# Down projection of a one-core decoder layer: the last pair of output tiles in block products too

## The chip, the cores and the metric

The kernel runs on one core of one Trainium2 chip. The metric is the device time of one execution in microseconds (us). Three executions of the kernel before took 895.30, 895.37 and 896.08 us; the median is 895.37 us.

## What is computed

The reference is one layer of a decoder: two token mixers side by side, then a convolutional FFN, for 512 prompt tokens and 8 sample tokens together (520 columns in the kernel). The change lies in the last part:

```python
a, gval = jnp.split(conv, 2, axis=-1)
x = x + (jax.nn.silu(a) * gval) @ w_down      # w_down: 2816 x 1024
...
y_prompt = rmsnorm(xp, g_final)
y_sample = rmsnorm(xs, g_final)
```

Everything is float32. The final RMS norm needs the sum of squares of each token over all 1024 features, so no output can be scaled before the last feature tile is finished.

## The kernel before

Activations lie feature-major: a tile is 128 features by 520 tokens, and the 1024 features make 8 tiles (`KT`). The down projection contracts 2816 hidden features, 22 k tiles (`FT`). Each 128 x 128 weight block is split in a high part (`whi`, written by ScalarE) and a low part (`wlo`, by VectorE), the activations likewise (`acth`, `actl`), and a k tile costs three matmuls for each stretch of columns: high by high, high by low, low by high. Two buffers `raw`, `whi`, `wlo` are used in turn; a "slot" is one weight load into one of them. SyncE issues the loads, each after the low part that used the buffer before.

**A pair.** `DownPair` treats two output tiles j and j+1. For k tiles 8 to 21 each is done directly, in two slots of 7 k tiles and two stretches of 260 columns (84 matmuls a tile). For k tiles 0 to 7 of both tiles together, a 2 x 2 block product (halves of 4 k tiles, halves of 260 columns) is formed in seven products of 12 matmuls in place of eight (Strassen-Winograd). VectorE makes four sums of weight blocks (`down_weight_sums`) in each pair; the sums of activations (`dth`, `dtl`) are made once. ScalarE and VectorE split the seven factors (`factor_hi`, `factor_low`), and VectorE puts the products together in the residual `x1`. Product 6 comes last; the last two slots of a pair, `n[6]` and `n[7]`, already hold the weights that TensorE needs next. `DOWN_PAIRS` is 3, so tiles 0 to 5 go this way.

**The last two tiles.** Tile 6 is done directly over all 22 k tiles in three slots (132 matmuls of 260 columns). Tile 7 is done in `last_tile` in two passes over the columns: pass 0 the 280 columns of `PARTS[0]`, pass 1 the other 240, with 66 matmuls each. Its third slot has buffers of its own (`whi_last`, `wlo_last`, written by `split_last` and `low_last`), since both passes need all weights.

**The end of the program.** Each engine works in program order.

- ScalarE, after its last split: six gained tiles `dn_gained(0)` to `(5)` (`xg` = `x1` times the gain; `xg` lies where `dth` was), `dn_square(6)`, `dn_gained(6)`, `table_of_sqrt` (loads the table of the square root), then `part_square(0)` (square of tile 7, first 280 columns), `part_gained(0)`, `part_root(0)`.
- VectorE: `dn_squares(6)` adds tile 6's squares to `acc`, `part_result(0)` adds pass 0 to `x1`, then the sum of squares (`sqa`, semaphore `s_sqs`), `part_scale(0)` (reciprocal), `part_y(0)` (five products of 280 columns into `y`), and only then `part_result(1)`, which adds pass 1.
- TensorE: inside pass 1, after its fifth k tile, `first_sums` (L2314) waits for `s_sqs` and sums the squares of the first 280 columns over the partitions. After pass 1 come four small matmuls over `acc`, four over `sqa` (after `part_square(1)`), and eight that spread the scale of the last 240 columns.
- GpSimd makes three tiles of `y` of the first part and two of the second; SyncE and ScalarE issue the stores.

Of the helpers, L581 is every ScalarE activation, L1961 every matmul, L1491 the low part of a factor, L1083 the low part of a slot, L1687 `dn_sum`, L1697 `dn_squares`, L1794 `part_result`, L1813 the sum of squares, L1809 `part_y`.

Of the kernel before, what the change touches and what calls it, by code (L numbers as in the profile page):

```python
# [17 lines left out]
F32 = mybir.dt.float32  # L18
F32R = mybir.dt.float32r
# [40 lines left out]
WHOLE = NC + 2  # L60
DOWN_PAIRS = 3
GATE_PAIRS = KT - WHOLE // 2
# [24 lines left out]
def hybrid_layer(nc, ins, outs):  # L87
    with ExitStack() as ctx:  # L88
# [5 lines left out]
        def at(name, shape, offset, dt=F32):  # L94

            return nc.alloc_sbuf_tensor_at(name, shape, dt, offset=base + offset)
# [4 lines left out]
        def sem(name):  # L101
            return ctx.enter_context(nc.semaphore(name))
# [40 lines left out]
        sct = at("sct", [P, 2 * FT, NB], F0 + 6688)  # L143
        LAST = (DN_CUTS[3] - DN_CUTS[2]) * P
        dth = at("dth", [P, 4, KT // 2, HALF], 0, F32R)
# [3 lines left out]
        dtmp = at("dtmp", [P, 2, HALF], F0 + 14880)  # L149
        whi_last = at("whi_last", [P, LAST], F0 + 6688, F32R)  # L150
        wlo_last = at("wlo_last", [P, LAST], F0 + 6688 + 4096, F32R)
        assert F0 + 19232 <= 6 * XB
# [141 lines left out]
        class DownPair(Pair):  # L294


            def __init__(self, i):
                self.q = GATE_PAIRS + i
                self.i, self.j = i, 2 * i
                self.n = [At(S_DN + 6 * i + t) for t in range(8)]  # L300
                self.t0, self.t1 = self.n[4].c % 2, self.n[5].c % 2
                self.p1, self.p6 = (trp[t][:, :, :].rearrange("p a b -> p (a b)")[:, 0:HALF] for t in range(2))
                self.p5, self.p7 = (aux[:, t, 0:HALF] for t in range(2))
                r0, r1 = raw[self.t0], raw[self.t1]
                self.a11, self.a12, self.a21, self.a22 = r0[:, 0:HW], r0[:, HW:], r1[:, 0:HW], r1[:, HW:]
                self.factor = (self.a11, self.a12, dsum[:, 3, :], dsum[:, 1, :], dsum[:, 0, :], dsum[:, 2, :], self.a22)
                self.next_width = down_width(0 if i == DOWN_PAIRS - 1 else 1)

        def down_width(g):

            return (DN_CUTS[g + 1] - DN_CUTS[g]) * P
# [128 lines left out]
        s_xg = sem("results_gained")  # L440
        s_wh = sem("last_slot_hi")
        s_wl = sem("last_slot_lo")
        s_half = sem("last_halves_done")
# [22 lines left out]
        def _(sp):  # L466
# [71 lines left out]
            def down_weights(j, g):  # L538

                return ins["w_dn"][j, :, DN_CUTS[g] * P:DN_CUTS[g + 1] * P]  # L540

            def down_slot(i, s):


                if i < DOWN_PAIRS:
                    return down_weights(2 * i + s // 2, 1 + s % 2), down_width(1 + s % 2)
                return down_weights(2 * i + s // 3, s % 3), down_width(s % 3)

            for s in range(4):
                load(At(S_DN + s), *down_slot(0, s))  # L550
            for pr in pairs_d:
                load(pr.n[4], down_weights(pr.j, 0))
                load(pr.n[5], down_weights(pr.j + 1, 0))
                src, width = down_slot(pr.i + 1, 0)
                sp.wait_ge(s_sw, 4 * pr.q + 4)
                sp.wait_ge(s_pl, 7 * pr.q + 2)
                sp.dma_start(raw[pr.t0][:, 0:width], src).then_inc(w_loaded[pr.t0], 16)
                src, width = down_slot(pr.i + 1, 1)
                sp.wait_ge(s_pl, 7 * pr.q + 7)
                sp.dma_start(raw[pr.t1][:, 0:width], src).then_inc(w_loaded[pr.t1], 16)  # L560
                for s in range(2, 4 if pr.i + 1 < DOWN_PAIRS else 6):
                    load(At(S_DN + 6 * (pr.i + 1) + s), *down_slot(pr.i + 1, s))
# [16 lines left out]
        def _(act):  # L579
            def A(out, in_, func=ACT.Copy, **kw_):  # L580
                return act.activation(out, in_, func, **kw_)  # L581
# [384 lines left out]

            def split_last():

                n = At(N_SLOTS - 1)
                act.wait_ge(w_loaded[n.c % 2], n.half(1) * 16)  # L970
                act.wait_ge(s_nc, 2 * FT)
                A(whi_last[:, :], raw[n.c % 2][:, 0:LAST]).then_inc(s_wh, 1)

            def dn_square(j):
# [14 lines left out]
            def down_pair(pr):  # L989
# [22 lines left out]
                A(whi[pr.t0][:, HW:pr.next_width], raw[pr.t0][:, HW:pr.next_width]).then_inc(w_hi, 3)  # L1012
                split(n[7], down_width(1 if pr is pairs_d[-1] else 2))

# [8 lines left out]
            for pr in pairs_d[1:]:  # L1023
                split(pr.n[2], down_width(1))
                dn_square(pr.j - 2)
                split(pr.n[3], down_width(2))
                dn_square(pr.j - 1)
                down_pair(pr)
            split(At(S_DN + 20), down_width(2))
            dn_square(4)  # L1030
            split(At(S_DN + 21), down_width(0))
            dn_square(5)
            split(At(S_DN + 22), down_width(1))
            split_last()
            for j in range(KT - 2):
# [40 lines left out]
        def _(dve):  # L1076
# [599 lines left out]

            def low_last():

                dve.wait_ge(s_wh, 1)
                TT(wlo_last[:, :], raw[(N_SLOTS - 1) % 2][:, 0:LAST], whi_last[:, :].bitcast(F32), ALU.subtract)\  # L1680
                    .then_inc(s_wl, 1)

            def dn_sum(j):
# [32 lines left out]
            def down_pair(pr):  # L1716
# [29 lines left out]
                result()  # L1746
                low(n[7], down_width(1 if pr is pairs_d[-1] else 2))
                ready(n[5])
                dn_sum(j + 1)
                dve.drain()  # L1750
# [4 lines left out]
                TT(part(1, 1), part(1, 1), dtmp[:, 0, :], ALU.add)  # L1755
                result()

# [15 lines left out]
            for pr in pairs_d[1:]:  # L1773
                low(pr.n[2], down_width(1))
                dn_squares(pr.j - 2)
                low(pr.n[3], down_width(2))
                dn_squares(pr.j - 1)
                down_pair(pr)
            low(At(S_DN + 20), down_width(2))
            dn_squares(4)  # L1780
            low(At(S_DN + 21), down_width(0))
            dn_squares(5)
            low(At(S_DN + 22), down_width(1))
            low_last()
            ready(At(S_DN + 20))
            dn_sum(6)
            result()
            dn_squares(6)
# [170 lines left out]
        def _(pe):  # L1959
# [333 lines left out]
            def down_pair(pr):  # L2293
                n, q = pr.n, pr.q
                banks = [(S_DN + t) % 2 for t in range(2)]
                for s in range(4):
                    t, g = s // 2, 1 + s % 2
                    if g == 1:
                        pe.wait_ge(evac[banks[t]], At(S_DN + pr.j + t).half(1))
                    down_slot(n[s], banks[t], g, g == 1, (1,) if s == 3 else (), q if pr.i > 0 and s == 0 else None, pr.i == 0 and t == 0)  # L2300
                if pr.i > 0:
# [9 lines left out]
                pe.wait_ge(s_tl, 4 + 4)  # L2311
                product(pr, 6, out_ps[banks[1]][:, 0, 0:HALF], *down_combination(3), first=False).then_inc(done, 2)

# [5 lines left out]
            def last_tile():  # L2319

                c = N_SLOTS - 3
                bank = (S_DN + 1) % 2
                pe.wait_ge(evac[bank], At(S_DN + 1, 3, 2).half(1))
                for a, h in enumerate(PARTS):
                    for q in range(3):
                        if a == 0 and q < 2:
                            pe.wait_ge(w_lo, c + q + 1)
                        if a == 0 and q == 2:
                            pe.wait_ge(s_wl, 1)
                        hi, lo = (whi[(c + q) % 2], wlo[(c + q) % 2]) if q < 2 else (whi_last, wlo_last)  # L2330
                        for k in range(DN_CUTS[q], DN_CUTS[q + 1]):
                            w = slice((k - DN_CUTS[q]) * P, (k - DN_CUTS[q] + 1) * P)
                            o = out_ps[bank][:, a, 0:h.stop - h.start]
                            MM(o, hi[:, w], acth[:, k, h], start=k == 0, stop=False)
                            MM(o, hi[:, w], actl[:, k, h], start=False, stop=False)
                            m = MM(o, lo[:, w], acth[:, k, h], start=False, stop=k == FT - 1)
                            if a == 1 and k == 4:
                                first_sums()
                    m.then_inc(s_half, 1)

            for pr in pairs_d:
                down_pair(pr)
            c = S_DN + 6 * DOWN_PAIRS
            pe.wait_ge(evac[S_DN % 2], At(S_DN + 2 * DOWN_PAIRS).half(1))
            down_slot(At(c), S_DN % 2, 0, True, (), pairs_d[-1].q + 1)
            down_slot(At(c + 1), S_DN % 2, 1, False, ())
            down_slot(At(c + 2), S_DN % 2, 2, False, (0, 1))
            last_tile()
# [100 lines left out]
```

## Time and profile before

| | before |
|---|---|
| three executions | 895.30, 895.37, 896.08 us |
| the profiled execution | 896.04 us |
| its span, first to last instruction | 894.20 us |
| TensorE busy | 886.6 us (99%), 7306 matmuls |
| VectorE busy | 609.9 us (68%) |
| ScalarE busy | 390.5 us (44%) |
| GpSimd busy | 133.0 us (15%) |
| mean granted TensorE clock | 0.996 |

Times in the views are counted from the start of the span. A matmul's own duration contains its way through the pipeline (280 ns and more for 260 columns), so the price of one in a row of many is the distance from start to start, not its duration. An activation, too, starts some 0.1 us before the one ahead of it ends. "idle before" is the time for which an engine did nothing ahead of an instruction, with the engine that released it.

### The profile page before, as it was taken

Reading aid. Unit: us, or ns where it says so; the run is one execution under the profiler, and the core shown is the slowest. Engines: PE = TensorE matmul, PEld = TensorE weight load, DVE = VectorE, ACT = ScalarE, POOL = GpSimd, SP = SyncE. Lnnn points to the kernel's source line nnn. Section 1 sums busy time; section 2 is a strip of 40 time slices with the busy share of each in tenths; the row PEclk is TensorE's granted clock in tenths of the full one; section 3 lists DMA queues with packets and bytes.
Section 4 is the critical chain, followed back from the end, with each engine's and each line's share of the span. In section 5 each row is a group of like instructions: output and inputs, shape, how many; then the busy total and the mean of one; then the engine's idle time right before and its main releaser. Section 6 shows DMA issues by size and latency. Waiting matters only on the chain.

```text
span 894.2 us, 18963 instructions
## 1 busy us (share of the span) xinstructions
PE 886.6 (99%) x7306; PEld 881.9 (99%) x7306; DVE 609.9 (68%) x980; ACT 390.5 (44%) x629; POOL 133.0 (15%) x182
## 2 busy tenths in 40 slices
PE   9999999999999999999999999999999999999997
PEld 9999999999999999999999999999999999999997
DVE  7886775443885568677755777777777778966543
ACT  7545434544873334344432344444444444432333
POOL 0673000002542110000005800000000000000001
PEclk9999999999999999999999999999999999999998
DMA  6332252234872222322255222222222222333232
GB/s 214 107 131 89 77 196 101 84 100 149 291 269 69 67 76 75 116 95 95 96 197 135 89 81 94 94 94 94 94 93 86 83 91 87 99 107 93 85 106 96
DMA packets 31499, 100.44 MB, mean 112 GB/s; under 512 B 4668, under 2 KB 7260, under 8 KB 31192
## 3 DMA queue, kind: packets, MB, share of 16 engines
q1 hardware_dynamic: 29256, 92.96, 31.1%
q0 software_dynamic: 1472, 5.72, 2.1%
q10 hardware_dynamic: 720, 1.04, 0.4%
q8 instruction: 36, 0.59, 0.3%
q14 instruction: 15, 0.12, 0.0%
HBM read 92.37 MB, written 7.35 MB: 112 GB/s over the span
## 4 chain that ended last, share of the span: by engine, by line
PE 91%; POOLq 3%; issue 3%; DMA 1%; POOL 1%; ACT 0%; SPq 0%; ACTq 0%
PE out L1961 84%; PE trp L1961 3%; PE aux L1961 2%; POOLq L1939 2%; POOLq L1937 1%; PE trp L1995 1%; DMA cwb<-in_conv_wb 1%; DMA raw_pair<-in_w_slots 1%; PE aux L2153 0%; POOL y L1952 0%; POOL out_conv_old L1923 0%; ACT xg L581 0%; POOL sct L1927 0%; POOLq L1930 0%; POOLq L88 0%
## 5 line engine op out<-in xcount | busy, mean ns | idle before, releaser
L581 ACT ACTIVATE whi<-raw_pair 128x1024 fp32r<-128x1024 f32 (+4 forms) x168 | 154.2, 924 | 207.4 <-PE out L1961 195.6
L1083 DVE TENSOR_TENSOR wlo<-raw_pair,whi 128x1024 fp32r<-128x1024 f32 (+1 forms) x121 | 155.2, 1282 | 86.8 <-ACT whi L581 86.4
L1961 PE MATMUL out<-xh,whi 128*128 128x260 f32 x668 | 143.5, 289 | 0.0
L1961 PE MATMUL out<-x2h,whi 128*128 128x260 f32 x704 | 141.8, 283 | 0.0
L1961 PE MATMUL out<-x2l,whi 128*128 128x260 f32 x704 | 141.3, 282 | 0.0
L1961 PE MATMUL out<-x2h,wlo 128*128 128x260 f32 x704 | 141.2, 282 | 0.0
L1961 PE MATMUL out<-xl,whi 128*128 128x260 f32 x668 | 139.0, 282 | 0.0
L1961 PE MATMUL out<-xh,wlo 128*128 128x260 f32 x668 | 139.0, 282 | 0.0
L1961 PEld LDWEIGHTS out<-x2h,whi 128*128 128x128 f32 x704 | 108.4, 188 | 0.1
L1961 PEld LDWEIGHTS out<-x2h,wlo 128*128 128x128 f32 x704 | 108.3, 188 | 0.0
L1961 PEld LDWEIGHTS out<-x2l,whi 128*128 128x128 f32 x704 | 108.3, 188 | 0.0
L1961 PEld LDWEIGHTS out<-xh,whi 128*128 128x128 f32 x668 | 105.2, 188 | 0.7 <-issue 0.2
L1961 PEld LDWEIGHTS out<-xl,whi 128*128 128x128 f32 x668 | 104.9, 188 | 0.0
L1961 PEld LDWEIGHTS out<-xh,wlo 128*128 128x128 f32 x668 | 104.9, 188 | 0.0
L1961 PE MATMUL out<-acth,whi 128*128 128x260 f32 (+2 forms) x266 | 58.2, 284 | 0.0
L1961 PE MATMUL out<-actl,whi 128*128 128x260 f32 (+2 forms) x266 | 57.8, 282 | 0.0
L1961 PE MATMUL out<-acth,wlo 128*128 128x260 f32 (+2 forms) x266 | 57.8, 282 | 0.0
L1645 DVE TENSOR_TENSOR up<-out,rbc 128x520 f32<-128x520 f32 x44 | 30.8, 700 | 37.5 <-PE out L1961 37.3
L1945 POOL COPY nconv<-up 128x10 f32 x44 | 10.4, 237 | 240.1 <-DVEq L1646 240.1
L581 ACT ACTIVATE acth<-silu 128x520 f32 (+1 forms) x22 | 14.1, 639 | 69.8 <-DVE silu L1660 69.8
L1961 PEld LDWEIGHTS out<-acth,whi 128*128 128x128 f32 x266 | 42.9, 188 | 0.2 <-DVE wlo L1491 0.2
L1961 PEld LDWEIGHTS out<-actl,whi 128*128 128x128 f32 x266 | 42.8, 188 | 0.0
(362 smaller groups left out, 1758.0 us busy)
## 6 DMA issues: line engine op xcount, KB each, us to landing
raw_pair<-in_w_slots SPq DMA_DIRECT2D x123, 512.0 KB, 3.3
raw_pair<-in_w_dn SPq DMA_DIRECT2D x16, 448.0 KB, 3.3
c_ring<-in_C_state SPq DMA_DIRECT2D x8, 512.0 KB, 5.1
row<-scratch SPq DMA_DIRECT2D x8, 512.0 KB, 5.9
out_C_sample<-c_ring SPq DMA_DIRECT2D x8, 512.0 KB, 4.3
raw_pair<-in_w_dn SPq DMA_DIRECT2D x8, 512.0 KB, 3.5
xres<-in_x_all POOLq DMA_DIRECT2D x1, 1560.0 KB, 6.8
x<-in_x_all SPq DMA_DIRECT2D x5, 260.0 KB, 6.7
```

The source lines that it names most:

```text
L581: return act.activation(out, in_, func, **kw_)
L1083: TT(wlo[p][:, 0:width], raw[p][:, 0:width], whi[p][:, 0:width].bitcast(F32), ALU.subtract)\
L1645: TT(both(up[t][:, 2:2 + TOK]), out2(n), both(rbc2[:, :]), ALU.mult).then_inc(evac[n.c % 2], 1)
L1937: pool.drain()
L1939: pool.drain()
L1945: pool.tensor_copy(nconv[:, i * 2 + t, :], up[t][:, SEQ:2 + TOK]).then_inc(s_nc, 1)
L1961: return pe.matmul(*a, **k)
L1995: m = pe.transpose(trp[b.c % 2][:, c, :], ftmp[b.c % 2][:, c * P:(c + 1) * P], ident[:, :])
```

## The change

`DOWN_PAIRS` becomes 4: k tiles 0 to 7 of tiles 6 and 7 are formed in seven block products too. Tile 6's k tiles 8 to 21 are done directly ahead of the products, in two slots that the third pair has split. Tile 7's k tiles 8 to 21 stay behind the products, in the two passes, with slots `n[6]` and `n[7]` of the last pair. Product 6 of the last pair goes to a bank of its own (`p4`, which is the bank of product 0) and VectorE adds it from there, since tile 7's bank isn't begun yet. The buffers `whi_last` and `wlo_last`, their two helpers and the three slots of tile 6 go. In the program order of ScalarE and VectorE, what stood between the third pair and the end (splits of slots 20 to 22, `split_last`) is replaced by the work of a pair, and the six gained tiles follow behind the last pair's `split(n[7])`. The diff, cut to its core:

```diff
-DOWN_PAIRS = 3
+DOWN_PAIRS = KT // 2
...
-                self.n = [At(S_DN + 6 * i + t) for t in range(8)]
+                self.last = i == DOWN_PAIRS - 1
+                self.n = [At(S_DN + 6 * i + t - (2 if self.last else 0)) for t in range(8)]
...
-                self.next_width = down_width(0 if i == DOWN_PAIRS - 1 else 1)
+                self.next_width = down_width(1)
+                self.p4 = self.p1 if self.last else out_ps[(S_DN + 1) % 2][:, 0, 0:HALF]
...
-                for s in range(2, 4 if pr.i + 1 < DOWN_PAIRS else 6):
+                for s in range(2, 4 if pr.i + 2 < DOWN_PAIRS else 2):
...
             for pr in pairs_d[1:]:
-                split(pr.n[2], down_width(1))
+                if not pr.last:
+                    split(pr.n[2], down_width(1))
                 dn_square(pr.j - 2)
-                split(pr.n[3], down_width(2))
+                if not pr.last:
+                    split(pr.n[3], down_width(2))
                 dn_square(pr.j - 1)
                 down_pair(pr)
-            split(At(S_DN + 20), down_width(2))
-            dn_square(4)
-            split(At(S_DN + 21), down_width(0))
-            dn_square(5)
-            split(At(S_DN + 22), down_width(1))
-            split_last()
             for j in range(KT - 2):
                 dn_gained(j)
             dn_square(6)
...
                 ready(n[5])
-                dn_sum(j + 1)
+                if pr.last:
+                    TT(part(1, 0), part(1, 0), pr.p4, ALU.add)
+                else:
+                    dn_sum(j + 1)
...
-            low(At(S_DN + 20), down_width(2))
-            dn_squares(4)
-            low(At(S_DN + 21), down_width(0))
-            dn_squares(5)
-            low(At(S_DN + 22), down_width(1))
-            low_last()
-            ready(At(S_DN + 20))
-            dn_sum(6)
-            result()
             dn_squares(6)
...
-                for s in range(4):
+                slots = n[2:4] if pr.last else n[0:4]
+                for s, m in enumerate(slots):
...
-                product(pr, 6, out_ps[banks[1]][:, 0, 0:HALF], *down_combination(3), first=False).then_inc(done, 2)
+                if pr.last:
+                    pe.wait_ge(s_dc, pr.i + 1)
+                product(pr, 6, pr.p4, *down_combination(3), first=pr.last).then_inc(done, 2)
...
                 for a, h in enumerate(PARTS):
-                    for q in range(3):
...
+                    for n, g in ((pr.n[6], 1), (pr.n[7], 2)):
+                        hi, lo = whi[n.c % 2], wlo[n.c % 2]
+                        for k in range(DN_CUTS[g], DN_CUTS[g + 1]):
+                            r = k - DN_CUTS[g]
+                            if a == 0 and r == (KT // 2 if g == 1 else 0):
+                                pe.wait_ge(w_lo, n(1))
...
-                            if a == 1 and k == 4:
+                            if a == 1 and k == DN_CUTS[1] + 4:
                                 first_sums()
...
-            down_slot(At(c), S_DN % 2, 0, True, (), pairs_d[-1].q + 1)
-            down_slot(At(c + 1), S_DN % 2, 1, False, ())
-            down_slot(At(c + 2), S_DN % 2, 2, False, (0, 1))
             last_tile()
```

## Rows read from the trace of the kernel before

**Rows 1.** The page, part 4: the chain that ended last, by line

```profile
PE out L1961 84%; PE trp L1961 3%; PE aux L1961 2%; POOLq L1939 2%; POOLq L1937 1%; PE trp L1995 1%; DMA cwb<-in_conv_wb 1%; DMA raw_pair<-in_w_slots 1%; PE aux L2153 0%; POOL y L1952 0%; POOL out_conv_old L1923 0%; ACT xg L581 0%; POOL sct L1927 0%; POOLq L1930 0%; POOLq L88 0%
```

**Rows 2.** Timeline of TensorE: start us, length us, engine, line, operation, count

```profile
842.94 0.28 PE L1961 MATMUL trp<-acth,whi 128*128 128x260 f32 x1
...
853.02 0.40 PE L1961 MATMUL out<-acth,whi 128*128 128x260 f32 x2
...
868.78 0.29 PE L1961 MATMUL out<-acth,whi 128*128 128x280 f32 x1
...
877.29 0.27 PE L1961 MATMUL out<-acth,whi 128*128 128x240 f32 x1
...
879.01 0.74 PE L1961 MATMUL aux<-sqa,ones 128*128 128x280 f32 x2
...
885.32 0.48 PE L1961 MATMUL out<-ones,acc 128*120 128x1 f32 x4
```

**Rows 3.** Timeline of ScalarE from the third pair's last split on

```profile
853.28 0.96 ACT L581 ACTIVATE whi<-raw_pair 128x896 fp32r<-128x896 f32 x1 [0.80 <-PE out L1961]
...
869.90 0.94 ACT L581 ACTIVATE whi_last<-raw_pair 128x896 fp32r<-128x896 f32 x1
870.74 3.81 ACT L581 ACTIVATE xg<-x,gains 128x520 f32<-128x520 f32 x6
874.46 0.62 ACT L581 ACTIVATE sqa<-x 128x520 f32<-128x520 f32 x1
...
875.71 1.28 ACT L581 ACT_TABLE_LOAD   x1
877.00 0.20 ACT L581 ACTIVATE unused<-eps 128x1 f32<-128x1 f32 x1
878.03 0.44 ACT L581 ACTIVATE sqa<-x 128x280 f32<-128x280 f32 x1 [0.83 <-DVE x L1794]
...
887.03 0.26 ACT L581 ACTIVATE nd<-out,eps 120x2 f32<-120x2 f32 x1 [0.67 <-PE out L1961]
```

**Rows 4.** Timeline of VectorE in the two passes and behind them

```profile
875.11 0.70 DVE L1697 TENSOR_TENSOR acc<-acc,sqa 128x520 f32<-128x520 f32 x1 [2.38 <-ACT sqa L581]
877.49 0.45 DVE L1794 TENSOR_TENSOR x<-out,x 128x280 f32<-128x280 f32 x1 [1.68 <-PE out L1961]
878.50 0.45 DVE L1813 TENSOR_TENSOR sqa<-sqa,acc 128x280 f32<-128x280 f32 x1 [0.56 <-ACT sqa L581]
...
882.76 1.87 DVE L1809 TENSOR_TENSOR y<-xg,aux 128x280 f32<-128x280 f32 x5 [0.54 <-ACT aux L581]
885.52 0.41 DVE L1794 TENSOR_TENSOR x<-out,x 128x240 f32<-128x240 f32 x1 [0.89 <-PE out L1961]
```

**Rows 5.** Timeline of VectorE in the third pair and behind it

```profile
838.85 1.29 DVE L1491 TENSOR_TENSOR wlo<-raw_pair,whi 128x512 fp32r<-128x512 f32 x2 [3.01 <-ACT whi L581]
...
843.86 0.69 DVE L1491 TENSOR_TENSOR wlo<-dsum,whi 128x512 fp32r<-128x512 f32 x1 [0.95 <-ACT whi L581]
...
854.27 1.09 DVE L1083 TENSOR_TENSOR wlo<-raw_pair,whi 128x896 fp32r<-128x896 f32 x1
...
857.08 0.43 DVE L1755 TENSOR_TENSOR x<-x,dtmp 128x260 f32<-128x260 f32 x1
```

**Rows 6.** The page, part 6: loads of 512 KB, us from issue to landing

```profile
raw_pair<-in_w_dn SPq DMA_DIRECT2D x8, 512.0 KB, 3.5
```

**Rows 7.** Windows at the end: stretch, busy time by engine, PEclk, DMA share, GB/s

```profile
887.00:887.50 0.50, 0.00 (x0) 0.00 (x0) 0.17 (x1) 0.47 (x2) 0.00 (x0) 1.00 1.02 349
887.50:888.00 0.50, 0.45 (x2) 0.45 (x3) 0.00 (x0) 0.17 (x1) 0.00 (x0) 0.57 1.05 365
...
889.00:889.50 0.50, 0.50 (x3) 0.33 (x2) 0.50 (x3) 0.00 (x0) 0.00 (x0) 0.50 0.00 0
```

**Rows 8.** Timeline of TensorE's weight loads behind pass 1

```profile
886.41 0.49 PEld L1961 LDWEIGHTS out<-ones,sqa 128*120 128x120 f32 x4 [0.70 <-ACT sqa L581]
...
888.36 0.97 PEld L1961 LDWEIGHTS trp<-ident,nd 120*128 120x128 f32 x4
```

More of the change, by code:

```diff
@@ L143, in hybrid_layer @@
         sct = at("sct", [P, 2 * FT, NB], F0 + 6688)
-        LAST = (DN_CUTS[3] - DN_CUTS[2]) * P
         dth = at("dth", [P, 4, KT // 2, HALF], 0, F32R)
@@ L149, in hybrid_layer @@
         dtmp = at("dtmp", [P, 2, HALF], F0 + 14880)
-        whi_last = at("whi_last", [P, LAST], F0 + 6688, F32R)
-        wlo_last = at("wlo_last", [P, LAST], F0 + 6688 + 4096, F32R)
         assert F0 + 19232 <= 6 * XB
@@ L440, in hybrid_layer @@
         s_xg = sem("results_gained")
-        s_wh = sem("last_slot_hi")
-        s_wl = sem("last_slot_lo")
         s_half = sem("last_halves_done")
@@ L542, in down_slot @@
             def down_slot(i, s):
-                if i < DOWN_PAIRS:
-                    return down_weights(2 * i + s // 2, 1 + s % 2), down_width(1 + s % 2)
-                return down_weights(2 * i + s // 3, s % 3), down_width(s % 3)
+                j = 2 * i + s // 2 if i < DOWN_PAIRS else KT - 1
+                return down_weights(j, 1 + s % 2), down_width(1 + s % 2)
             for s in range(4):
@@ L964, in _ @@
             up_step(FT - 1, last=True)
[L967 to L972, printed above, removed]
             def dn_square(j):
@@ L1012, in down_pair @@
                 A(whi[pr.t0][:, HW:pr.next_width], raw[pr.t0][:, HW:pr.next_width]).then_inc(w_hi, 3)
-                split(n[7], down_width(1 if pr is pairs_d[-1] else 2))
+                split(n[7], down_width(2))
             split(At(S_DN + 2), down_width(1))
@@ L1675, in _ @@
             hidden_low(FT - 1)
[L1677 to L1681, printed above, removed]
             def dn_sum(j):
@@ L1746, in down_pair @@
                 result()
-                low(n[7], down_width(1 if pr is pairs_d[-1] else 2))
+                low(n[7], down_width(2))
                 ready(n[5])
-                dn_sum(j + 1)
+                if pr.last:
+                    TT(part(1, 0), part(1, 0), pr.p4, ALU.add)
+                else:
+                    dn_sum(j + 1)
                 dve.drain()
@@ L1755, in down_pair @@
                 TT(part(1, 1), part(1, 1), dtmp[:, 0, :], ALU.add)
-                result()
+                if not pr.last:
+                    result()
             dve.wait_ge(s_nc, 2 * FT)
@@ L1773, in _ @@
             for pr in pairs_d[1:]:
-                low(pr.n[2], down_width(1))
+                if not pr.last:
+                    low(pr.n[2], down_width(1))
                 dn_squares(pr.j - 2)
-                low(pr.n[3], down_width(2))
+                if not pr.last:
+                    low(pr.n[3], down_width(2))
                 dn_squares(pr.j - 1)
                 down_pair(pr)
-            low(At(S_DN + 20), down_width(2))
-            dn_squares(4)
-            low(At(S_DN + 21), down_width(0))
-            dn_squares(5)
-            low(At(S_DN + 22), down_width(1))
-            low_last()
-            ready(At(S_DN + 20))
-            dn_sum(6)
-            result()
             dn_squares(6)
@@ L2299, in down_pair @@
                         pe.wait_ge(evac[banks[t]], At(S_DN + pr.j + t).half(1))
-                    down_slot(n[s], banks[t], g, g == 1, (1,) if s == 3 else (), q if pr.i > 0 and s == 0 else None, pr.i == 0 and t == 0)
+                    down_slot(m, banks[t], g, g == 1, (1,) if s == 3 else (), q if pr.i > 0 and s == 0 else None, pr.i == 0 and t == 0)
                 if pr.i > 0:
@@ L2319, in last_tile @@
             def last_tile():
-                c = N_SLOTS - 3
+                pr = pairs_d[-1]
                 bank = (S_DN + 1) % 2
+                pe.wait_ge(s_nl, pr.q + 1)
                 pe.wait_ge(evac[bank], At(S_DN + 1, 3, 2).half(1))
                 for a, h in enumerate(PARTS):
-                    for q in range(3):
[L2326 to L2332, printed above, removed]
+                    for n, g in ((pr.n[6], 1), (pr.n[7], 2)):
[4 more added lines that the diff above has]
+                                pe.wait_ge(w_lo, n(1))
+                            w = slice(r * P, (r + 1) * P)
                             o = out_ps[bank][:, a, 0:h.stop - h.start]
-                            MM(o, hi[:, w], acth[:, k, h], start=k == 0, stop=False)
+                            MM(o, hi[:, w], acth[:, k, h], start=k == DN_CUTS[1], stop=False)
                             MM(o, hi[:, w], actl[:, k, h], start=False, stop=False)
                             m = MM(o, lo[:, w], acth[:, k, h], start=False, stop=k == FT - 1)
-                            if a == 1 and k == 4:
+                            if a == 1 and k == DN_CUTS[1] + 4:
                                 first_sums()
@@ L2342, in _ @@
                 down_pair(pr)
-            c = S_DN + 6 * DOWN_PAIRS
-            pe.wait_ge(evac[S_DN % 2], At(S_DN + 2 * DOWN_PAIRS).half(1))
-            down_slot(At(c), S_DN % 2, 0, True, (), pairs_d[-1].q + 1)
-            down_slot(At(c + 1), S_DN % 2, 1, False, ())
-            down_slot(At(c + 2), S_DN % 2, 2, False, (0, 1))
             last_tile()
```

## The prediction

> **What bounds the kernel now.** I read the page's chain of work that ended last first: matmuls carry nearly all of it [rows 1]. So a matmul removed is worth its full distance from start to start, as long as TensorE is what ends last where it is removed. The second view asks that for the place of the change, the end: the timelines of TensorE, ScalarE and VectorE side by side. In the trace before, TensorE starts tile 6 at 853.02, pass 0 of tile 7 at 868.78, pass 1 at 877.29 and the small sums behind it at 885.32, with `first_sums` at 879.01 inside [rows 2]. ScalarE is ready for `part_square(0)` early: it ends the square root's dummy at 877.20 and idles 0.83 until VectorE has added pass 0 [rows 3]. VectorE ends `part_y(0)` at 884.63 and idles 0.89 until pass 1 is done, then starts `part_result(1)` at 885.52 [rows 4]. So the reader is to see that TensorE is last at both ends, but with only 0.83 and 0.89 to spare, against a change that takes more than that from TensorE just there.
>
> **TensorE's own work.** Matmuls of 260 columns follow each other at (868.78 - 853.02) / 132 = 0.1194, those of 280 at (877.29 - 868.78) / 66 = 0.1289, those of 240 at (879.01 - 877.29) / 15 = 0.1147, a little high [rows 2]. Removed: tile 6's 132 and tile 7's 66 + 66. Added: 84 of 260 for tile 6, the seven products, and 42 + 42 for tile 7. The third pair's products took 853.02 - 842.94 = 10.08. Tile 7 now begins, call it T0, at 853.02 + 84 x 0.1194 + 10.08 = 873.13. Pass 0 lasts 42 x 0.1289 = 5.41, to 878.54. Pass 1 with its sums lasted 885.32 - 877.29 = 8.03 and loses 24 x 0.1147 = 2.75, so it would end at 883.82. **Left to itself TensorE gains 1.50**, twelve matmuls.
>
> **Will the last pair's operands be there?** Its loads are those of any pair. The factors' loads are issued behind the low parts of the third pair's last slots, the later one at 855.36 [rows 5]; with 3.5 for 512 KB [rows 6] it lands by 859, while VectorE asks for it with its weight sums, after 860. In program order the squares of tiles 4 and 5 now stand directly before the pair. VectorE ends tile 5 at 857.51, adds a square (0.70, [rows 4]), ScalarE squares tile 5 (0.62, [rows 3]), VectorE adds it: about 859.65. The first low part of a factor would start at 838.85 + 20.11 = 858.96 if this were the third pair moved on by the distance between the products' starts (863.05 - 842.94). So VectorE is 0.7 late, and behind its weight sums it had 0.95 to spare [rows 5]. Cost nothing; with the cover gone it is 0.1 or so. Product 6's added wait is for a copy made five products earlier: nothing, and only tile 7 stands behind it. The bank of its own costs VectorE an addition of 260 columns in place of one of 520.
>
> **The last slot.** `n[7]` can be split only once product 6 is done, and pass 0 wants it after 21 matmuls, at T0 + 2.71. In the third pair the split starts at 853.28, 0.26 after the products, and its low part ends at 855.36, T0 + 2.34 [rows 3, 5]. It fits by 0.37. If it didn't, pass 0 would wait a few tenths, and by the next paragraph even that would be hidden.
>
> **ScalarE's end, which is moved.** Before, the six gained tiles start at 870.74, beside pass 0, already 6.6 ahead of its end. Now they stand behind `split(n[7])`, so behind product 6. Split at T0 + 0.26 = 873.39, with 0.96 less the 0.10 of overlap that 869.90 + 0.94 against 870.74 shows: the gained tiles start at 874.25. Six take 874.46 - 870.74 = 3.72, to 877.97. Square and gain of tile 6 take 875.71 - 874.46 = 1.25, to 879.22; the table load 1.29, to 880.51; the dummy about 0.14 more [rows 3]. `part_square(0)` starts at 880.65, not 878.03. VectorE isn't the later one: its square of tile 6 is added 0.65 after ScalarE starts it, 878.62 to 879.32, and `part_result(0)` then allows the square at about 879.94 [rows 4].
>
> A rule speaks against this point. The Trainium skill, ScalarE: Activation LUTs, section "What ACT_TABLE_LOAD costs", gives a switch of tables 1283 ns for the load and about 1380 ns for a drain. The load agrees with the row of 1.28; no such drain stands between it and the dummy there. If it came behind the dummy, the sum would be later by 1.38 by that section.
>
> **What waits for that.** From the square to `first_sums` it was 879.01 - 878.03 = 0.98, so `first_sums` runs at 881.63. TensorE gets there at 878.54 + 15 x 0.1147 = 880.26 and waits 1.37, with the rest of pass 1 queued behind. That rest was 885.32 - 879.01 = 6.31 and is now 6.31 - 24 x 0.1147 = 3.56: pass 1 ends at 885.19, where it ended before. The gain is gone. Worse is VectorE: from `first_sums` to the first product of `part_y(0)` it took 882.76 - 879.01 = 3.75 (root, reciprocal, copy), and five products take about 1.82 [rows 4]. `part_result(1)`, queued behind them, can't start before 881.63 + 3.75 + 1.82 = 887.20. It started at 885.52: **1.68 later**. The serial chain behind it moves as a whole. The stores of the first part move too, by 2.6; they had ended by 889.0 [rows 7] and would end by 891.6, while the second part's data began to move after 890 and now begin after 891.7. Nothing, or a few tenths.
>
> **The clock.** Granted clock was 1.00 until 887.5 and 0.57 in the next half microsecond, so it fell to 0.50 (1.2 GHz) at about 887.57, 2.25 after the last dense matmul [rows 7]. The four sums over `sqa` at 886.41 still ran at 2.4 GHz; their weight loads took 0.49, where four later ones at 1.2 GHz took 0.97 [rows 8]. They move to 888.09, 2.9 after the last dense matmul. Between 0 and 0.48 I take the whole 0.48, as the rows put the fall before them. The eight matmuls that spread the scale were slow already.
>
> **Sum.** 1.68 + 0.48 = 2.16. Against the profiled execution, span 894.20 and 1.84 around it, that is 898.2. That execution lies 0.67 above the median, and I forecast for the median: 895.37 + 2.16 = **897.5**.
>
> **The rivals.**
> - **The same, with the clock still up** in the four sums, because the fall isn't tied to the last dense matmul: 895.37 + 1.68 = 897.05. Chance 0.20. A difference of 0.2% is 1.79 here, about what a measurement can tell from none; this case lies just inside it.
> - **ScalarE's chain is hidden** (not slower): part of the gains and the table load runs beside product 6, or the chain is otherwise at least 1.4 shorter, so `first_sums` runs at 880.26. That is the point from which it decides: from there on TensorE's own arrival sets `first_sums`, and VectorE's 3.75 + 1.82 behind it end at 885.83, 0.3 later than before. The clock's term falls away for the most part. Price +0.3: 895.7. For it speaks that everything ahead of the square is plain work; against it, the program order and the wait for product 6. Chance 0.12.
> - **ScalarE stalls behind the table load.** The 0.83 of idle before the square [rows 3] can cover a stall of up to that length; it would come on top: 898.3. The load itself is followed by the dummy without a gap, which counts against it. Chance 0.07. The drain that the Trainium skill states (ScalarE: Activation LUTs, "What ACT_TABLE_LOAD costs") would look like this here.
> - **The clock falls in TensorE's new wait** of 1.37. 24 to 27 matmuls of 240 columns would take twice as long, and pass 1 would end near 888.2, 1 behind VectorE: 898.8. Against it: 2.25 passed before the fall at the end [rows 7]. Chance 0.05.
> - **The full 1.50**: 893.9. `part_result(1)` would have to overtake `part_y(0)`, and program order forbids it. With all else by which the change does other than it says, 0.04, half of it below.
>
> The forecast has 0.52.
>
> **Range and chances.** The range goes from 896.4 to 898.9: it holds the forecast, the clock's two ends, the stall and the clock in the wait, and leaves out the hidden chain and the full gain. Slower by over 0.2% (above 897.16): 0.50 of the forecast, the stall, the clock in the wait, and little of the second case, 0.62. Faster by over 0.2% (below 893.58): 0.03. Within: 0.35.
>
> **What the profile after would show.** Tile 7 starting near 873.1, with no wait in the pair. ScalarE without idle from 873.4 to `part_square(0)` at 880.7. A wait of 1.4 in TensorE before `first_sums`, released by VectorE's sum. `part_result(1)` directly behind `part_y(0)`, at 887.2, no longer released by TensorE. Weight loads of the sums over `sqa` of 0.97. I am wrong if ScalarE idles before `part_square(0)`, if `part_result(1)` is still released by TensorE, or if a wait appears in the products of the last pair.

## The result, and the profile after

The changed kernel takes 897.66 us (median of 8 runs, 896.99 to 900.01), the kernel before 895.66 (8 runs, 895.08 to 896.80): a ratio of 1.0025, 95% interval 1.0015 to 1.0036, so 1.3 to 3.2 us slower, 2.0 by the medians. The forecast was 897.5.

The profiled execution of after has a span of 897.8 and took 899.68, which is 2.0 above its median. Before anything is compared, that has to be taken out. The first matmuls of the two kernels, which are the same code, show it. Timeline of TensorE near the start, before:

```profile
7.17 0.66 PE L1961 MATMUL out<-xul,whi 128*128 128x260 f32 x4
7.66 0.66 PE L1961 MATMUL out<-xuh,wlo 128*128 128x260 f32 x4
```

and after:

```profile
7.47 1.07 PE L1937 MATMUL out<-xul,whi 128*128 128x260 f32 x4
8.34 1.07 PE L1937 MATMUL out<-xuh,wlo 128*128 128x260 f32 x4
```

Four matmuls follow four others after 0.49 before and after 0.87 in after, until about 10.8 us. By 16 us the same instructions lie 1.8 later in after, by 356 us 2.15, all of it in code that the two kernels share. The low part of the third pair's last slot starts at 854.27 before [rows 5] and at 856.39 after. I call this instruction the mark and compare distances from it.

TensorE after, from tile 7's first matmul on (start, length, engine, line, operation):

```profile
875.27 0.29 PE L1937 MATMUL out<-acth,whi 128*128 128x280 f32 x1
...
880.66 0.27 PE L1937 MATMUL out<-acth,whi 128*128 128x240 f32 x1
...
883.72 0.74 PE L1937 MATMUL aux<-sqa,ones 128*128 128x280 f32 x2 [1.21 <-DVE sqa L1789]
...
887.32 0.48 PE L1937 MATMUL out<-ones,acc 128*120 128x1 f32 x4
```

ScalarE after, from the last pair's split of `n[7]` on:

```profile
875.53 0.95 ACT L577 ACTIVATE whi<-raw_pair 128x896 fp32r<-128x896 f32 x1 [0.91 <-PE trp L1937]
876.39 3.82 ACT L577 ACTIVATE xg<-x,gains 128x520 f32<-128x520 f32 x6
880.11 0.62 ACT L577 ACTIVATE sqa<-x 128x520 f32<-128x520 f32 x1
880.64 0.71 ACT L577 ACTIVATE xg<-x,gains 128x520 f32<-128x520 f32 x1
881.36 1.28 ACT L577 ACT_TABLE_LOAD   x1
882.65 0.20 ACT L577 ACTIVATE unused<-eps 128x1 f32<-128x1 f32 x1
882.76 0.42 ACT L577 ACTIVATE sqa<-x 128x280 f32<-128x280 f32 x1
```

VectorE after, in the third pair's tail, the last pair, and the end:

```profile
856.39 1.09 DVE L1068 TENSOR_TENSOR wlo<-raw_pair,whi 128x896 fp32r<-128x896 f32 x1 [0.38 <-ACT whi L577]
...
862.01 1.29 DVE L1476 TENSOR_TENSOR wlo<-raw_pair,whi 128x512 fp32r<-128x512 f32 x2
...
866.17 2.02 DVE L1476 TENSOR_TENSOR wlo<-dsum,whi 128x512 fp32r<-128x512 f32 x3
...
876.51 1.09 DVE L1068 TENSOR_TENSOR wlo<-raw_pair,whi 128x896 fp32r<-128x896 f32 x1 [0.38 <-ACT whi L577]
...
883.21 0.45 DVE L1789 TENSOR_TENSOR sqa<-sqa,acc 128x280 f32<-128x280 f32 x1 [1.21 <-ACT sqa L577]
...
887.47 1.87 DVE L1785 TENSOR_TENSOR y<-xg,aux 128x280 f32<-128x280 f32 x5 [0.55 <-ACT aux L577]
889.26 0.40 DVE L1770 TENSOR_TENSOR x<-out,x 128x240 f32<-128x240 f32 x1
```

What the reader is to see. TensorE has a wait that it didn't have before: 1.21 before `first_sums`, released by VectorE. ScalarE runs without any idle from 875.53 to the square at 882.76, where it had 0.83 to spare before [rows 3]. `part_result(1)` at 889.26 has no idle ahead of it and no releaser: it stands directly behind the five products, where it had waited 0.89 for TensorE before [rows 4].

The six stores of `y` that SyncE issues (SPq), before and after; the group starts with the first store of the first 280 columns:

```profile
884.66 6.75 SPq L566 DMA_DIRECT2D out_y<-y  x6
```

```profile
889.37 5.67 SPq L562 DMA_DIRECT2D out_y<-y  x6
```

The clock and the small sums after (windows: stretch, busy time by engine, PEclk, DMA share, GB/s; then TensorE's weight loads):

```profile
890.50:891.00 0.50, 0.22 (x3) 0.14 (x2) 0.00 (x0) 0.24 (x2) 0.00 (x0) 1.00 0.99 349
891.00:892.00 1.00, 0.72 (x4) 0.72 (x5) 0.17 (x1) 0.41 (x2) 0.00 (x0) 0.71 1.02 346
```

```profile
890.14 0.49 PEld L1937 LDWEIGHTS out<-ones,sqa 128*120 128x120 f32 x4 [2.44 <-ACT sqa L577]
...
891.99 0.97 PEld L1937 LDWEIGHTS trp<-ident,nd 120*128 120x128 f32 x4
```

The granted clock fell at about 891.4, 4.2 after the start of the last dense matmul (887.20), and the sums over `sqa` ran at 2.4 GHz as before.

### The profile page after: what moved, and what is told of

The parts are those of the page before. It is cut to its first block, busy times and chain, and to the rows that moved or that the text cites. A ratio compares the mean times of both kernels' runs of the same rounds, so it can differ in the third digit from the quotient of the medians.

```text
span 897.8 us, 18983 instructions
## 1 busy us (share of the span) xinstructions
PE 887.0 (99%) x7294; PEld 881.9 (98%) x7294; DVE 618.3 (69%) x999; ACT 393.1 (44%) x636; POOL 132.1 (15%) x182
## 4 chain that ended last, share of the span: by engine, by line
PE 89%; POOLq 3%; issue 3%; DMA 2%; DVE 2%; POOL 1%; DVEq 0%; ACT 0%; SPq 0%; ACTq 0%
PE out L1937 81%; PE trp L1937 4%; PE aux L1937 3%; POOLq L1915 2%; POOLq L1913 1%; DMA raw_pair<-in_w_slots 1%; PE trp L1971 1%; DMA cwb<-in_conv_wb 1%; PE aux L2129 0%; DVE wlo L1068 0%; DVE tf L1410 0%; DVE tl L1415 0%; POOL y L1928 0%; DVE tf L1406 0%; POOL out_conv_old L1899 0%
## 5 line engine op out<-in xcount | busy, mean ns | idle before, releaser
L1068 DVE TENSOR_TENSOR wlo<-raw_pair,whi 128x1024 fp32r<-128x1024 f32 (+1 forms) x119 | 152.5, 1282 | 78.9 <-ACT whi L577 78.6
```

The lines of the kernel that those rows point to most:

```text
L1068: TT(wlo[p][:, 0:width], raw[p][:, 0:width], whi[p][:, 0:width].bitcast(F32), ALU.subtract)\
```

## The experiments

All times of this table are from the profiled executions, counted from the mark of each; the medians are of the timed runs. The kernel before had medians of 895.83 to 895.86 beside them (26 to 33 runs).

| kernel | median | first_sums | part_result(1) | first store | end |
|---|---|---|---|---|---|
| before | 895.66 | 24.74 | 31.25 | 30.39 | 39.9 |
| after | 897.66 | 27.33 | 32.87 | 32.98 | 41.4 |
| e1, ScalarE's order | 896.42 | 25.99 | 31.53 | 31.64 | 40.3 |
| e2, VectorE's order | 897.71 | 27.33 | 31.25 | 33.59 | 41.8 |
| e3, both orders | 896.27 | 26.00 | 29.89 | 32.24 | 40.4 |
| e4, before, VectorE's order | 897.90 | 24.75 | 31.35 | 33.70 | 41.9 |
| e5, gains twice | 901.90 | 31.04 | 37.14 | 37.25 | 45.5 |
| e6, before, gains twice | 898.72 | 27.52 | 34.03 | 33.17 | 42.8 |
| e7, both orders, stores in pieces | 895.18 | 26.00 | 30.11 | 30.90 | 39.1 |
| e8, e2 without first stores | 895.54 | 27.32 | 31.22 | none | 39.4 |
| e9, after without first stores | 897.60 | 27.33 | 32.87 | none | 41.3 |
| e10, before, busy end | 895.57 | 24.74 | 31.25 | 30.39 | 39.4 |
| e11, after, busy end | 897.44 | 27.32 | 32.86 | 32.97 | 41.2 |
| e12, all | 894.79 | 25.99 | 30.11 | 30.22 | 38.7 |

My theory: ScalarE's chain sets `first_sums`, and `part_result(1)` is held up by the products that stand before it. The rivals: the cost lies in the last pair or the small matmuls; or the stores, which moved later, bound the end.

**e1: ScalarE's order.** The seven gained tiles are spread around the square, into stretches where ScalarE had waited.

```diff
-            for j in range(KT - 2):
-                dn_gained(j)
             dn_square(6)
-            dn_gained(6)
             table_of_sqrt()
-            act.nop().then_inc(s_xg, 1)
+            for j in range(4):
+                dn_gained(j)
             act.wait_ge(s_accf, KT)
...
             part_square(0)
-            part_gained(0)
+            dn_gained(4)
             part_root(0)      # inside, between root and copy: dn_gained(5), dn_gained(6), part_gained(0)
```

> The changed kernel, with only ScalarE's program order behind its last split altered: square of tile 6, square-root table and dummy, four gained tiles, then part_square(0); the fifth gained tile behind it, the sixth and seventh while VectorE takes the reciprocal. Theory (ScalarE's chain holds up first_sums): the wait of 1.2 us in TensorE before first_sums goes, first_sums comes 1.37 earlier against tile 7's start (7.1 instead of 8.45), part_result(1) still stands directly behind part_y(0), and the kernel is 1.4 us faster than the change: near 896.3, 0.3 above the kernel before. Rival (something else, the last pair's products or the small matmuls, costs the time): no gain, near 897.7.

Measured: 896.42, that is 1.24 less than the change and 0.6 above the kernel before beside it (ratio 1.0007, 0.9998 to 1.0016, so not told from it). `first_sums` of e1:

```profile
880.26 0.74 PE L1938 MATMUL aux<-sqa,ones 128*128 128x280 f32 x2
```

The wait before `first_sums` is gone and it comes 1.34 earlier; `part_result(1)` is still directly behind the products, 0.28 later than before the change. That is what the theory expected: of the 2.0 us, ScalarE's chain is 1.1 (to the end of the traces) to 1.3.

**e2 and e4: VectorE's order, in the changed kernel and in the kernel before.**

```diff
             part_scale(0)
-            part_y(0)
             part_result(1)
+            part_y(0, 0, 4)
             dve.wait_ge(s_stdf, 2)
             dve.reciprocal(nd[0:CH, 1, 0:2], nd[0:CH, 0, 0:2]).then_inc(s_dg, 1)
+            part_y(0, 4, Y_DVE[0])
```

> The changed kernel, with only VectorE's order altered: part_result(1) directly behind part_scale(0), four products of part_y(0), the small reciprocal, the fifth product. TensorE's wait before first_sums stays. Theory (part_result(1) is late because five products stand ahead of it): it starts 1.8 us earlier, where part_y(0) started, 3.75 behind first_sums, and the kernel takes near 895.9, equal to the kernel before. Rival (TensorE's late pass 1 alone holds part_result(1)): pass 1 ends 3.6 behind first_sums already in the changed kernel, so no gain would be seen if the products were not in the way: near 897.7.

> The kernel before with VectorE's new order only. Theory: there part_result(1) is released by TensorE with 0.9 of idle ahead of it, so the order is worth nothing: within 0.2 us of the kernel before, 895.7. Rival (the new order helps any kernel, and e2 and e3 say nothing about the change): 1.5 us or more faster here too.

Measured: e2 897.71, no gain (ratio to the kernel before 1.0021, 1.0012 to 1.0030); e4 897.90, 2.0 slower than the kernel before (1.0024, 1.0015 to 1.0033). Both against what I expected. e2 lies on the number of its rival, but not for the rival's reason: `part_result(1)` came 1.62 earlier, where it stood before the change, and is released by TensorE again:

```profile
885.33 0.41 DVE L1770 TENSOR_TENSOR x<-out,x 128x240 f32<-128x240 f32 x1 [0.72 <-PE out L1938]
```

e4 shows what I had left out. Timelines of VectorE, GpSimd and SyncE of e4:

```profile
885.36 0.41 DVE L1794 TENSOR_TENSOR x<-out,x 128x240 f32<-128x240 f32 x1 [3.40 <-PE out L1962]
885.68 1.51 DVE L1809 TENSOR_TENSOR y<-xg,aux 128x280 f32<-128x280 f32 x4
```

```profile
889.03 1.34 POOL L1953 TENSOR_TENSOR y<-xg,ftmp 128x240 f32<-128x240 f32 x2 [4.71 <-ACT ftmp L581]
```

```profile
887.71 5.42 SPq L566 DMA_DIRECT2D out_y<-y  x6
```

VectorE idles 3.40 for pass 1, with five products of the first part queued behind it that could have been made in this time. The first part's stores are issued at 887.71, 3.3 later from the mark than before, and the end comes 2.0 later although GpSimd's last products start 0.8 earlier from the mark. In e2, e3 and e4 the end is 8.2 behind the first store (33.59 to 41.8, 32.24 to 40.4, 33.70 to 41.9), where it was 9.5 in the kernel before. So the new hypothesis is: y's stores need 8.2 from their first issue, and the order traded a wait for that.

**e3: both orders.**

> The changed kernel with both new orders. Theory: the two delays lie on one chain, so their gains add: 1.4 + 1.8 = 3.2 less than the change, and TensorE is last at both ends again; 1.5 us below the kernel before (twelve matmuls), near 894.2. Rival (the gains overlap, since either order alone makes the room): near 895.9, like the better of the two alone.

Measured: 896.27 (1.0005, 0.9996 to 1.0014), 0.15 below e1 and 1.4 below e2. The gains don't add, but not for the rival's reason: `part_result(1)` did come 2.98 earlier than in the change, and the stores took it back: the end is 8.2 behind the first one.

**e8 and e9: without the stores of the first 280 columns**, in e2 and in the change. The four lines that wait for this part and issue its stores are left out.

> e2 (VectorE's new order in the changed kernel) without the stores of the first 280 columns of y: the kernel leaves that part of the output unwritten. Theory (e2's gain of 1.8 us was taken back by the stores, whose first is issued at the end of part_y(0), 8.2 before the end): without them the end follows GpSimd's last products by the 4.1 of the kernel before, 2.3 us less than e2: near 895.4. Rival (VectorE's order brings nothing by itself): 897.7, like e2.

> The changed kernel without the stores of the first 280 columns of y, which it leaves unwritten. Theory (in the change itself the products of the last columns, not the stores, come last: 4.1 from GpSimd's last products to the end, as before the change): within 0.3 us of the change, 897.4 to 897.7. Rival (the stores that moved 2.6 later already bound the change, and the prediction hit its number by a second cause): 1 us or more faster.

Measured: e8 895.54, 2.2 below e2: the stores are what took e2's gain. e9 897.60, 0.06 below the change: there they cost nothing. The change itself is bound by its last products, as predicted, but with little room: its first store comes 8.4 before the end (32.98 to 41.4), and 8.2 is the least.

A second distance tells the two bounds apart: from VectorE's first product of the last 240 columns to the end it is 5.4 in the kernel before, in the change, in e1, e8 and e9, and 7.3 to 7.8 in e2, e3 and e4, where the stores come last.

**e5 and e6: ScalarE's chain longer by six activations**, in the change and in the kernel before.

```diff
             for j in range(KT - 2):
                 dn_gained(j)
+                A(y[:, j, :], x1[:, j, :], scale=gains[:, 3, j:j + 1])
```

> The changed kernel with each of the six gained tiles accompanied by a second activation of the same size (written to y, which is overwritten later), so ScalarE's chain is 3.72 us longer. Theory (that chain sets first_sums, and everything behind it is serial): TensorE waits 3.7 longer before first_sums and the whole kernel is 3.7 us slower than the change, near 901.4. Rival (the stores or another chain bound the end): less than 2.

> The kernel before with the same six extra activations as in e5 (3.72 us of ScalarE behind its last split). Theory (there the chain ended 0.83 before the data of part_square(0), so the first 0.8 is covered): part_square(0) 2.9 later, TensorE waits 2.9 before first_sums, the kernel 2.9 us slower than itself, near 898.7, against the 4.2 that e5 cost the change. Rival (the chain isn't what counts): within 1 us.

Measured: e5 901.90 (1.0069, 1.0053 to 1.0084), 4.2 above the change; e6 898.72 (1.0038, 1.0025 to 1.0051; its five runs lie between 898.0 and 900.4), 2.9 above the kernel before. `first_sums` moved by 3.71 in e5 and by 2.78 in e6. The difference, 0.93, is the cover that the kernel before had and the change has spent (I read 0.83 of idle in [rows 3]). In e5 `part_result(1)` moved by 0.56 more than `first_sums`, and its trace has the reason. `first_sums` of e6, then `first_sums` and two windows of e5:

```profile
881.51 0.74 PE L1962 MATMUL aux<-sqa,ones 128*128 128x280 f32 x2 [2.66 <-DVE sqa L1814]
```

```profile
884.87 1.30 PE L1938 MATMUL aux<-sqa,ones 128*128 128x280 f32 x2 [4.92 <-DVE sqa L1790]
```

```profile
884.00:885.00 1.00, 0.13 (x1) 0.13 (x1) 0.45 (x1) 0.75 (x3) 0.00 (x0) 0.87 0.03 8
885.00:886.00 1.00, 1.00 (x3) 0.74 (x4) 0.00 (x0) 0.00 (x0) 0.00 (x0) 0.50 0.00 0
```

The clock fell in a wait of 4.92, shortly before its end, and the sums took 1.30 in place of 0.74. This is what the prediction's fourth rival describes: it happened in the wait of 4.92 here and not in the wait of 2.66 in e6, where the clock is still 1.00. In the change the wait is 1.21, and the clock stays up. The end of e5 moved by 4.1, less than `part_result(1)` with 4.3: the clock was up again in the spread, but the end is 8.2 behind the first store, so the stores bound it too.

**e10 and e11: TensorE kept busy in its last waits**, in the kernel before and in the change.

```diff
+            keep_busy(6)     # matmuls of 128 columns into a free bank; 24 in e11
             pe.wait_ge(s_sqf, KT + 1)
...
+            keep_busy(6)
             pe.wait_ge(s_dg, 1)
```

> The kernel before with twelve matmuls of 128 columns into an unused bank in TensorE's last two waits (six before the sums over sqa, six before the spread of the scale), so that it is never idle for long before the spread. Theory (the granted clock falls in these waits, and the eight spreading matmuls at 1.2 GHz lie on the path): the clock stays at 2.4 GHz through the spread, which takes 1.1 to 1.2 us in place of 2.1, and the kernel is 0.5 to 1.0 us faster, near 895.1. Rival (the clock's fall is hidden, or falls all the same): 895.8.

> The changed kernel with thirty such matmuls in the same two waits (24 and 6, as its first wait is 2.4 us). Theory (the first part's stores leave it little room: its first store comes 8.4 before the end, and 8.2 was the least in e2, e3 and e4): the clock stays up, the spread is shorter, but at most 0.3 us is gained: near 897.4. Rival (the stores are not near the bound in the change): as much as in the kernel before, 0.5 to 1.0, near 896.9.

Measured: e10 895.57 against 895.83, ratio 0.9996 (0.9987 to 1.0005): not told from no change by the timed runs, though its trace ends 0.5 earlier from the mark. e11 897.44 against 897.66, also within the spread (ratio to before 1.0017, 1.0008 to 1.0026), 0.2 in the trace. In both the clock stayed up through the spread. e11's number is the theory's, but its trace has another cause than the stores. TensorE and VectorE of e11:

```profile
889.78 0.53 PE L1937 MATMUL out<-ones,sqa 128*120 128x1 f32 x4
891.60 1.98 DVE L1785 TENSOR_TENSOR y<-xg,aux 128x240 f32<-128x240 f32 x6 [0.80 <-PE aux L1937]
```

The 24 added matmuls ran past the wait that they were to fill, so the sums over `sqa` came 0.25 later from the mark than in the change (34.00 for 33.75) and VectorE's last products only 0.21 earlier. They begin 5.4 before the end, as in the change, so the end followed them; how near the stores are to the bound in the change, e11 doesn't test. TensorE of e10:

```profile
887.21 0.69 PE L1961 MATMUL aux<-ident,nd 120*128 120x120 f32 x4
887.74 0.61 PE L1961 MATMUL trp<-ident,nd 120*128 120x120 f32 x4
```

Before they took 1.21 and 1.06. So the clock's fall costs the end some 0.5 in an execution where it comes ahead of the spread, and there are executions where it doesn't: in e4, e5 and e8, without an added matmul in these waits, the spread ran at 2.4 GHz.

**e7 and e12: a version that leaves the stores room.** e1's order on ScalarE; on VectorE one product, `part_result(1)`, three products, the small reciprocal, the fifth; the first part stored in three pieces as its tiles come (five in e12, the first after one tile), and in e12 fourteen matmuls in TensorE's last waits.

```diff
-            sp.wait_ge(s_y, Y_DVE[0])
-            store_y(0, 0, Y_DVE[0])
+            sp.wait_ge(s_y, 2)
+            store_y(0, 0, 2)
             sp.wait_ge(s_yp, KT - Y_DVE[0])
             store_y(0, Y_DVE[0], KT)
+            sp.wait_ge(s_y, Y_DVE[0])
+            store_y(0, 2, Y_DVE[0])
```

> ScalarE's order of e1; on VectorE one product of part_y(0) ahead of part_result(1), three behind it, the small reciprocal, the fifth; and SyncE stores the first part in three pieces, the first as soon as two tiles of y are there. Theory (e2, e3 and e4 were bound by the stores: their first store was issued 8.2 before the end in each): the first store starts near 1.3 before that of e3, VectorE and GpSimd end 0.3 later than in e3, and the kernel ends 1.2 to 1.4 us before e3, near 895.0, below the kernel before. Rival (the stores of the last 240 columns cost the time by themselves, however early the first part leaves): no better than e3, 896.3.

> e7 with the first part's stores in five pieces, the first when one tile of y is there, and with fourteen matmuls in TensorE's last waits. Theory (e7 is bound by the stores from 886.65 on): the first store leaves 0.7 earlier and the kernel ends up to 0.7 earlier, near 894.5, faster than the kernel before by 1.3. Rival (the stores of the last columns, two of them on ScalarE's queue, bound e7): 895.2, like e7.

Measured: e7 895.18 (ratio to before 0.9996, 0.9987 to 1.0005), 1.1 below e3 and 2.5 below the change. e12 894.79 (0.9988, 0.9979 to 0.9997), 1.0 below the kernel before: the only version whose interval lies below it. DMA engines of e7, in 40 slices from 884 to 895 (busy tenths, then GB/s), and the stores' issue in e12:

```profile
DMA  0000000000000999999999999999999999940000
GB/s 0 0 0 0 0 0 0 0 0 0 0 0 20 346 326 354 379 367 350 391 330 334 338 346 320 322 360 339 370 339 297 311 311 363 377 157 0 0 0 0
```

```profile
884.55 5.29 SPq L562 DMA_DIRECT2D out_y<-y  x9
```

In e7 the DMA engines have no gap between the first store and the last, and VectorE's last products begin 5.7 before the end where 5.4 would do: it is bound by what it has to write. e12 starts writing 0.7 earlier and ends 0.4 earlier, 8.45 behind its first store. Windows of e12:

```profile
885.50:886.00 0.50, 0.50 (x6) 0.50 (x7) 0.40 (x2) 0.05 (x1) 0.39 (x1) 1.00 0.85 298
886.00:886.50 0.50, 0.50 (x7) 0.50 (x6) 0.26 (x2) 0.50 (x2) 0.00 (x0) 1.00 0.65 226
```

The DMA engines were not full there (shares of 0.85 and 0.65, some 0.25 us unused), probably because only the first pieces were ready. VectorE's last products begin 5.8 before the end, so the stores bind e12 as well, and by the shares most of the lost 0.3 lies in this gap. e12 combines two things; what its added matmuls bring by themselves, no run tells.

## Why the prediction was right, point by point

**TensorE's own work: right.** Tile 7 began 18.88 behind the mark (875.27 - 856.39); the prediction has 18.86 (873.13 - 854.27). The last pair ran without a wait. From there pass 0 took 5.39 for the predicted 5.41. The twelve matmuls fewer are there, 1.5 us, and are spent later.

**The last pair's operands: right, with less cover than worked out.** VectorE's low parts of the first factors start 5.62 behind the mark (862.01), where the prediction has 5.38 (859.65). That is 0.9 late, not 0.7, and the 0.95 of idle before the factors of sums [rows 5] is gone: at 866.17 no idle is shown. TensorE didn't notice, as the product that needs them comes later, but this cover is spent.

**The last slot: right.** Its low part starts at 876.51, T0 + 1.24, and ends at T0 + 2.33, for the predicted 2.34.

**ScalarE's chain: right.** The square starts at T0 + 7.49 (882.76 - 875.27); predicted T0 + 7.52. e1, e5 and e6 show that it decides. The drain behind the table load that would have made the third rival isn't there: the dummy starts 1.29 after the load and the square 0.11 after the dummy. The Trainium skill, ScalarE: Activation LUTs, section "What ACT_TABLE_LOAD costs", gives 1283 ns for the load, and the trace agrees (1.28); of the 1380 ns of drain that it adds, this trace shows nothing.

**What waits for it: right.** TensorE's wait is 1.21 (predicted 1.37), `part_result(1)` is 1.62 later from the mark (predicted 1.68). Taking away either delay moved `part_result(1)` back: by 1.34 in e1 (the wait), by 1.62 in e2, where TensorE is last there again. e1 also gives what the second rival, the hidden chain, would have cost: `first_sums` at 25.99 from the mark is its 880.26, and `part_result(1)` is 0.28 later than before, for its +0.3.

**The stores: right in this kernel, wrong as an argument.** "Nothing, or a few tenths" holds (e9: 0.06). But I compared when the first part's data would be written with when the second's would begin, and found room of a tenth. What I didn't see is how near that is to a bound: with 8.2 from the first store to the end, the change has 0.2 left. My expectations of e2, e3 and e4, which I built on the same sum, were too low by 1.8, 2.1 and 2.2 us for it.

**The clock: the term that was mis-sized.** I took the fall, which before came 2.25 after the last dense matmul, as tied to it, and put 0.48 on the sums over `sqa`. In the profiled execution of after the fall came 4.2 after, and the term was 0. So the weight loads of these sums took 0.49, where 0.97 had been given as a sign. The eight spreading matmuls ran at 1.2 GHz in both, as forecast, but for the first of them in after, which brought VectorE's last products forward by 0.1. Over the profiles of the kernels without added matmuls in these waits, the distance from the last dense matmul's start to the fall was between 2.3 (e6) and 5.2 (e4); in the kernel before it was 2.4, as the 2.25 counts from the sums that follow. In e1 the fall did reach these sums (0.71 in place of 0.58 for the four). One row of one execution was a draw, not a rule.

**The sum.** 1.68 + 0.48 = 2.16 was forecast; the traces differ from the mark to the end by 41.4 - 39.9 = 1.5, the medians by 2.0 (1.3 to 3.2), or 1.8 against the 895.84 that the kernel before had in the later runs. Of the 1.62 by which `part_result(1)` moved, 0.1 came back in the spread. So the mechanism stands for 1.5. The other 0.3 to 0.5 isn't explained by the traces: it may be the clock's term in a share of the executions, and it may be the spread of the runs. That part of the forecast's closeness may be luck.

## What to carry to other kernels

Where work is taken from the engine that ends last, list what else has to be done between the change and the end, on every engine and on the stores, with the idle time that each had. Here these were 0.83 and 0.89, against 1.50 taken from TensorE: the gain can't be larger than the smallest of them, and what is moved behind the shortened stretch is lost on top. A step that others wait for (here a square) must not stand in program order behind work that only the end needs (here the gained tiles). And when a reduction of the tail is tried, send out finished data in pieces as early as it exists; otherwise the bytes of the output become the next bound.

## What the hardware showed that I had not expected

- The granted clock's fall came anywhere from 2.3 to 5.2 us behind the last dense matmul in executions of nearly the same code.
- The start varies too, with four matmuls in 0.87 in place of 0.49 until about 10.8 us. By an estimate that is the 1.2 GHz level: e5 at a clock of 0.50 has 240 columns every 0.213, so 260 would take 0.23, near the 0.22 here. The clock's row reads 1.00 there in both kernels, so the cause isn't shown. It moved the profile of after by 1.8 of its 2.1 us and is as large as the effect under study; only distances from a common mark make such traces comparable.
- A wait of TensorE of 2.66 (e6) left the clock at 1.00; in one of 4.92 (e5) it fell.
- Where the 2.1 MB of `y` come last, the end is 8.2 us behind the issue of their first store (e2, e3, e4, e5 and, with smaller pieces, e7), with the DMA engines busy from the first data to the last (e7: 297 to 391 GB/s).
